# The first pair of weight steps of each feed-forward layer computed without the seven-product scheme

## The reference, cut to what matters

```python
def swiglu(u, wg, wu, wd):
    return (jax.nn.silu(u @ wg) * (u @ wu)) @ wd

for l in range(DEPTH):                       # DEPTH = 2
    hp = hp + 0.5 * swiglu(rms_norm(hp, norm_ffn1[l]), ffn1_wg[l], ffn1_wu[l], ffn1_wd[l])
    ...
    hp = hp + mp                             # mixer A and B in layer 0, a pooling mixer in layer 1
    hp = hp + 0.5 * swiglu(rms_norm(hp, norm_ffn2[l]), ffn2_wg[l], ffn2_wu[l], ffn2_wd[l])
```

## Time and profile before

| | before |
|---|---|
| median of 3 runs | 1993.95 us (1992.81 to 1995.24) |
| span of the profiled execution | 1990.5 us |
| PE busy | 1886.5 us, 95% |
| DVE / ACT / POOL busy | 69% / 61% / 41% |
| matmuls | 14529 |

### The profile page before, as it was taken

How to read it: one execution, slowest core, us unless ns; L and a number is a source line. 1 busy time by engine, 2 the same in 40 slices (tenths; PEclk the granted TensorE clock), 3 DMA queues, 4 the chain that set the end, 5 groups by cost and what they waited for, 6 DMA issues and landing times. The chain is left out here.

```text
span 1990.5 us, 37093 instructions
## 1 busy us (share of the span) xinstructions
PE 1886.5 (95%) x14529; PEld 1431.9 (72%) x14531; DVE 1377.3 (69%) x2159; ACT 1220.6 (61%) x1509; POOL 813.3 (41%) x520
## 2 busy tenths in 40 slices
PE   5999999999999889899999998999999989999999
PEld 2677777776668747677777775777777667777777
DVE  8767863467998866777876367768753787788532
ACT  5677787744933375577785346777743347778631
POOL 5666521112545132566640046666300457675000
PEclk8999999999999999999999999999999999999999
DMA  3222337612110021122222221223322012232330
GB/s 146 85 106 85 106 141 266 255 47 75 59 43 26 35 85 43 43 97 93 106 101 92 87 82 64 87 103 106 123 97 79 22 46 106 106 107 93 117 115 22
DMA packets 29170, 183.96 MB, mean 92 GB/s; under 512 B 3600, under 2 KB 4080, under 8 KB 13440
## 3 DMA queue, kind: packets, MB, share of 16 engines
q1 hardware_dynamic: 22896, 161.08, 22.6%
q0 software_dynamic: 6160, 21.34, 2.9%
HBM read 178.58 MB, written 3.83 MB: 92 GB/s over the span
## 5 line engine op out<-in xcount | busy, mean ns | idle before, releaser
L2404 PE MATMUL ps<-big 128*128 128x296 f16 (+1 forms) x2464 | 717.2, 291 | 31.3 <-DVE big L1535 12.0
L2410 PE MATMUL ps<-big 128*128 128x296 f16 (+1 forms) x2464 | 716.8, 291 | 15.8 <-DVE big L1412 14.3
L2405 PE MATMUL ps<-big 128*128 128x296 f16 (+1 forms) x2464 | 716.8, 291 | 0.0
L2386 PE MATMUL ps<-big 128*128 128x296 f16 (+1 forms) x4296 | 549.1, 290 | 7.6 <-POOL big L551 3.3
L2386 PEld LDWEIGHTS ps<-big 128*128 128x128 f16 x4296 | 415.4, 98 | 132.7 <-DVE big L1543 4.4
L467 POOL TENSOR_TENSOR big<-big 128x512 f32<-128x512 f32 x88 | 122.0, 1386 | 500.4 <-ACT big L734 245.8
L2404 PEld LDWEIGHTS ps<-big 128*128 128x128 f16 x2464 | 242.1, 98 | 111.1 <-DVE big L1535 15.0
L2410 PEld LDWEIGHTS ps<-big 128*128 128x128 f16 x2464 | 242.0, 98 | 92.5 <-DVE big L1412 21.2
L2405 PEld LDWEIGHTS ps<-big 128*128 128x128 f16 x2464 | 242.3, 98 | 66.2 <-issue 0.3
L1535 DVE SCALAR_TENSOR_TENSOR big<-big,scales 128x2048 f16<-128x2048 f32 x88 | 246.3, 2799 | 9.8 <-ACT big L753 9.4
L745 ACT ACTIVATE big<-big,scales 128x1536 f16<-128x1536 f32 x88 | 138.6, 1575 | 181.1 <-PE ps L2410 132.2
(11 more groups left out here) (354 smaller groups left out, 2636.9 us busy)
## 6 DMA issues: line engine op xcount, KB each, us to landing
big<-in_w_up SPq DMA_DIRECT2D x88, 1024.0 KB, 4.7
big<-in_w_dn SPq DMA_DIRECT2D x32, 1408.0 KB, 5.9
big<-in_w_in POOLq DMA_DIRECT2D x20, 512.0 KB, 6.0
big<-in_w_in SPq DMA_DIRECT2D x20, 512.0 KB, 3.3
big<-in_w_out POOLq DMA_DIRECT2D x8, 512.0 KB, 6.3
big<-in_w_out SPq DMA_DIRECT2D x1, 4096.0 KB, 12.1
resid<-in_x SPq DMA_DIRECT2D x4, 592.0 KB, 6.1
out_y<-resid SPq DMA_DIRECT2D x8, 296.0 KB, 4.7
```

The source lines that it names most:

```text
L2386: last = mm(ps[:, bank + hf, 0:n], w, x[:, hf * HALF:hf * HALF + n], start=start, stop=stop)
L2404: mm(out, w[:, 0, c], xop[:, 0, x, c, 0:FFN_COLS[f]], start=start, stop=False, skip_group_check=True)
L2405: mm(out, w[:, 1, c], xop[:, 0, x, c, 0:FFN_COLS[f]], start=False, stop=False, skip_group_check=True)
L2410: last = mm(out, w[:, 0, c], xop[:, 1, x, c, 0:FFN_COLS[f]], start=False, stop=(c == DC // 2 - 1), skip_group_check=True)
```

## The change

`FAST` stays for pairs 1 to 10. The first pair (steps u=0 and u=1) no longer uses the seven products. Each step is now 4 quarters x 2 token halves = 8 half-size products of 12 matmuls, 96 per step and 192 per pair instead of 168. PE's new function `plain` runs them:

```diff
+                def plain(h, b, groups, signal=None, n=0):
+
+                    w = w16[:, b, :, 0:4 * QW].rearrange("p a (q c n) -> p a q c n", q=4, c=DC // 2)
+                    out = [ps[:, bank, 0:FFN_COLS[f]] for bank in ((0, 2), (3, 4), (5, 6), (3, 4))[2 * h + b]]
+                    for g in groups:
+                        side, k = g // 2, g % 2
+                        x = (7, 3)[side] if h else side
...
+                        if h and b and g == 0:
+                            pe.wait_ge(hid1_done, PAIRS * f + 1)
+                            pe.wait_ge(hid2_done, PAIRS * f + 1)
+                        pe.wait_ge(x_high, 16 * f + X_AT[x] + k + 1)
+                        for c in (2 * k, 2 * k + 1):
...
+                            for m in range(2):
+                                for part in range(2):
+                                    mm(out[m], w[:, part, PLAIN[m, side], c], high, start=(g == 0 and c == 0 and part == 0),
+                                       stop=False)
+                        low_wait(f, x, k)
+                        for c in (2 * k, 2 * k + 1):
...
-                halves = stage != 0
-                order = [(0, "P1"), (0, "P2"), (1, "P1"), (1, "P2")] if stage in (3, 5) else \
-                    [(0, "P1"), (1, "P1"), (0, "P2"), (1, "P2")]
...
-                    first_step(b, name)
-                unit_total(stage, 3, 1)
-                with pe.Fori(1, HEAD_PAIRS) as i:
+                plain(0, 0, (0, 1))
+                if stage:
+                    sums(stage, 1)
+                plain(0, 1, (0, 1))
+                if stage:
+                    spread_half(stage, 1)
+                plain(0, 0, (2, 3), prod_done[0], 3)
+                plain(0, 1, (2, 3), prod_done[1], 3)
+                plain(1, 0, (0, 1))
+                plain(1, 1, (0, 1))
+                plain(1, 0, (2, 3), prod_done[0], 4)
+                unit_total(stage, 2, 0)
+                plain(1, 1, (2, 3), prod_done[1], 4)
+                pe.wait_ge(silu_done, PAIRS * f + 1)
+                unit_total(stage, 3, 1)
+                pair(1)
+                with pe.Fori(2, HEAD_PAIRS) as i:
                     pair(i)
```

The first argument of `plain` is the token half, the second the step (0 gate, 1 up); groups 0 and 1 are feature chunks 0 to 3, groups 2 and 3 chunks 4 to 7. The second token half of the up step shares banks 3 and 4 with the first half, so it waits until DVE has multiplied them out. The 24 `idle_products` are gone. Around this, on the other engines:

```diff
 # POOL
             def ffn(stage, next_stage=None):
 
-                if stage:
-                    first_lows(FFN_OF_STAGE[stage])
+                first_lows(FFN_OF_STAGE[stage])
                 mix_weights(stage, 2, 0)
                 mix_x(FFN_OF_STAGE[stage])
-                for u in range(3, FC):
+                mix_weights(stage, 3, 1)
+                mixed_low(FFN_OF_STAGE[stage])
+                for u in range(4, FC):
                     mix_weights(stage, u, u % 2)
...
-                if next_stage:
-                    first_two(next_stage)
 # ACT, first_turn
-                for b in range(2):
-                    if b or stage == 0:
-                        seed_p1(f, 0, b, FIRST)
-                x_highs(f, 2)
+                x_highs(f, 7)
                 x_highs(f, 3)
...
-                silu_first(f, 0, FIRST)
-                for b in range(2):
-                    keep_p5(f, 0, b, FIRST)
+                x_highs(f, 2)
+                plain_silu(f, 0)
                 x_highs(f, 4)
                 x_highs(f, 5)
-                keep_u2(f, 0, 0, FIRST)
+                bound(stage, 3, 1)
+                plain_silu(f, 1)
+                step_high1(stage, 2, 0)
+                step_high2(stage, 2, 0)
                 x_highs(f, 6)
...
 # DVE, x_rest
-                for k in range(2):
-                    scale_x(stage, 2 * k, 1)
-                    scale_x(stage, 2 * k + 1, 1)
-                    mix(0, k)
...
+                for c in range(DC):
+                    scale_x(stage, c, 1)
...
+                for k in range(2):
+                    x_low_of(stage, 3, k)
+                for t in range(2):
+                    for k in range(2):
+                        mix(t, k)
+                for k in range(2):
+                    x_low_of(stage, 2, k)
+                plain_hidden(f, 0)
+                for k in range(2):
+                    mix(2, k)
+                for k in range(2):
+                    x_low_of(stage, 4, k)
+                weight_scale(stage, 2, 0)
+                step_low1(stage, 2, 0)
+                step_low2(stage, 2, 0)
+                for k in range(2):
+                    x_low_of(stage, 5, k)
```

More of the change, by code:

```diff
@@ L744, in step_high1 @@
                     act.wait_ge(part_mm, DC * f - 1 + u)
-                a.activation(w16[:, b, 0, 0:3 * QW], wslot[:, b, QW:STEP_W], ACT.Copy, scale=wscale[:, b:b + 1]) \
+                first = 0 if isinstance(u, int) and u < 2 else QW
+                a.activation(w16[:, b, 0, 0:3 * QW], wslot[:, b, first:first + 3 * QW], ACT.Copy, scale=wscale[:, b:b + 1]) \
                     .then_inc(whigh1_done, 1)
@@ L2306, in _ @@
             step_low1(5, 0, 0)
+            step_low2(5, 0, 0)
             def next_updates():
```

226 lines of the change are left out of this document (120 added, 106 removed).

## The result

The changed kernel takes **2021.9 us** (median of 4 runs, 2021.0 to 2023.1) where the kernel before takes 1993.7 in the same comparison: a ratio of **1.0142 (95% interval 1.0127 to 1.0156)**, slower by 28 us. I had forecast 1982.7. The profiled execution has a span of 2019.8 us against 1990.5, 29.3 us more, and it is this difference that is taken apart here.

The account below looks back on a forecast made before the run. PE was taken to bound the kernel, 95% busy, with gains in the FFN heads, ended by ACT/DVE weight preparation. Heads: 11.1 - 1.6 + 3.5 + 3.4 = 16.4, less 5.1 for clock: 1993.95 - 11.3 = 1982.7 us, range 1973 to 1993.

Parts of the forecast that it names:

- waits for banks 3 and 4: PE's new wait before the up step's second token half, until DVE's plain_hidden: 3.4 us in FFN 1 to 3, 0.4 in FFN 0.
- low clock, behind the waits and behind E: Three more low-clock stretches of 3.4 us over the heads, half lost each: 5.1 us. E is P6's first matmul, pair 1.
- the four tails: From step 0's last product to E (P6's first matmul, pair 1): 12.3 us per head, 11.8 in FFN 3.
- T0 of FFN 0: First product of FFN 0's head: at 22.0 us, 2.5 earlier than before.
- Eight operations on x: 7.8 us: DVE's work ahead of freeing the banks: four low parts at 1.10 us and four sums at 0.85, the earlier group means.
- POOL has only four sums and two low parts there: Argument against DVE and POOL taking turns at the eight operations ahead of the banks.
- the slower rival: DVE and POOL take turns at the eight operations, 1.97 us each; wait 7.9 us longer per head, 2014 us; chance 0.10.
- Two low parts of operand 5: 2.0 us: DVE's low parts, new in the tail between step_low2 of step 2 and the scale of step 3: 2.0 us.
- from E on nothing differs: Sign for the new profile: no change after E, the first matmul of P6 in pair 1, step 0.
- a low stretch lasts 3.4 us: Expected length of PE's low-clock stretches, half of it lost each time; bounds none and 3.4 us per head.
- The head of FFN 1: From first product T0 to E: 25.6 + 12.3 = 37.9 us against 36.3 before, 1.6 lost.
- the twelve us of products: 24 added matmuls in each of four first pairs, 0.126 us each: 12.1 us more PE work, against the waits.

Follow-up runs that it names:

- e11: Changed kernel with one line moved: POOL forms step 2's sums ahead of operand 7's low parts, with no new wait; 2010.5 us.
- e2: Changed kernel with one wait more: POOL starts step 2's sums only after the first pair's SiLU products (hid2_done); 1993.6 us.
- e3: Changed kernel with weight_back of step 2 and the scale of step 3 on DVE ahead of operand 5's low parts and the memset; 2009.3 us.
- e6: Changed kernel with the edits of e2 and e3 together; 1984.7 us.
- e10: e6 with POOL's step 2 sums ahead of operand 7's low parts, step 3's ahead of mix_x, and SiLU products ahead of operand 2's low parts; 1981.2 us.
- e7: e6 with POOL's sums of step 3 also delayed, until behind step_low2 of step 2; 1990.0 us.
- e8: e7 with SiLU products right behind DVE's first two low parts, and POOL waiting for x's fourth low part instead of the products; 1997.7 us.

## Why the prediction was wrong

The forecast's span was 1990.5 - 11.3 = 1979.2 us, the measured one 2019.8: 40.6 us apart. In the forecast's own terms:

| term | forecast | measured | difference |
|---|---|---|---|
| waits for banks 3 and 4 (0.4 + 3 x 3.4) | 10.6 | 32.3 | +21.7 |
| low clock, behind the waits and behind E | 5.1 | 16.2 | +11.1 |
| the four tails | 48.7 | 53.6 | +4.9 |
| T0 of FFN 0, and the way to the banks | | | +0.9 |
| stretches that the change does not touch | 0 | 1.8 | +1.8 |

The lines add up to 40.4; the rest is rounding.

- **"Eight operations on x: 7.8 us" is the term that failed.** It measured 13.0 (1.62 us each, above the 1.33 from which the change was said to lose). The means of the earlier trace rows came from heads in which POOL stood idle, or was itself held, beside most of these operations. They are means over operations at full pace (0.72 to 0.78 us, as 814.98 above) and operations that took turns with POOL (up to 1.97), and I used them without asking which of the two the new place would be. The wait of PE followed one for one: 8.5 instead of 3.4 us, and 6.8 instead of 0.4 in FFN 0.
- **"POOL has only four sums and two low parts there" was the reason given against the slower rival, and it did not count against it.** Four sums of step 2, two sums of x and the end of a low part, with turns on each, cover all eight operations. I had not followed POOL's queue past the new `first_lows`, although the row of its idle time and the line of the diff were both at hand. e11 puts the sums back and regains 4.3 us in the eight; e2 takes all of POOL but operand 7's low parts away and regains 6.8.
- **The slower rival had the mechanism right and the size nearly.** It said turns at 1.97 us, a wait 7.9 us longer, and 2014 us. It was 5.1 us longer in three heads and 6.4 in FFN 0. The time went above 2014 through what the rival left out: operand 5's low parts and the clock. A chance of 0.10 was too low for it. The rule of the Trainium skill (SBUF — State Buffer, Who interferes with whom) would have made this rival the forecast. The trace agrees with the rule in direction, with 13.0 us beside POOL against 6.2 in e2, where only operand 7's low parts stand beside the first of the eight. It does not show a complete exclusion, and it shows DVE at full pace beside POOL as well (814.98 in the kernel before): from 820.22 to 825.53 us POOL did three sums (3.8 us at 1.26) and DVE about three and a half operations (2.6 us at 0.73), together 6.4 us of work in 5.3, an estimate from the rows above. The scalings, with one input in PSUM, kept to 3.56 us for eight beside POOL's 2.58 us of low parts, as it also says.
- **"Two low parts of operand 5: 2.0 us"** measured 3.67, by the same error. With the rest of the tail near its forecast (step_low1 1.82 for 2.1, step_low2 2.35 for 2.7), the tail of FFN 1 was 853.20 - 839.62 = 13.6 us for 12.3.
- **The clock** was forecast at 5.1 us and cost 16.2. In FFN 1 the first twelve matmuls behind the wait ran at the 1.2 GHz level (0.246 us apart) and cost 1.9 us with what followed; behind the four waits it was 7.5 us together, behind the four E 8.7. The second place was the wrong one: I expected "from E on nothing differs". PE had idled 5.09 us in front of E, and in e3, where it idles 0.94, the clock behind E stays high. That a low stretch lasts 3.4 us was a size without a row: the earlier trace rows show one low stretch, of 6.80 us. What it was meant to price, 1.7 us per place, measured 1.3 to 2.7.
- The head of FFN 1 in these terms: 37.9 forecast + 5.1 (wait) + 1.9 (clock behind it) + 1.3 (tail) = 46.2; measured 46.28. The rest stood: T0 of FFN 0 at 22.75 (forecast 22.0), PE at the banks 16.3 us behind T0 (16.2), the scalings' start, and the twelve us of products that were to be paid for out of the old waits: e2, with every product of the change, is level with the kernel before, and e6 and e10 are below it.
- The wait alone does not mend the forecast. In e2 PE waits 5.4 us for the banks, less than the 10.6 forecast, and its time of 1993.6 is still 11 us above 1982.7. The tail had to be shortened too: e6 comes to 1984.7.

What stays open: 1.8 us of the difference lie in stretches with the same code. Why DVE and POOL take turns in one place and one of them is held in another isn't shown. A kernel in which POOL's sums of steps 2 and 3 both stand in its idle time wasn't tried; in FFN 0 and 2 the load of step 2 has only just landed there.

## What to carry to other kernels

A mean duration from a profile belongs to its neighbours. Before an operation of DVE with both inputs in SBUF is priced in a new place, lay POOL's timeline beside that place. In this kernel such an operation of 592 columns was worth 0.75 us where POOL was idle; where POOL worked it was anything from 0.72 us, with POOL held, to 1.97, and the forecast has to carry both ends as its range. When a helper at the front of an in-order queue gets an operand that comes later, everything behind it moves too; look for what had used the idle time. And give each experiment that delays one engine the question of when its own results are due: e7 and e8 lost to that.

## What the runs showed that I had not expected

One sum of POOL took 5.16 us while DVE ran six operations at full pace, and in the changed kernel both engines were slowed (POOL 1.6 to 1.8 us for 1.26, DVE 1.6 for 0.75). The runs do not show what decides between the two. In e10 POOL's sum began 0.15 us behind an operation of DVE both times: in FFN 1 it was held over six operations, in FFN 0 the engines took turns from the second operation on. In e2 POOL began 0.16 us behind DVE (818.88 and 818.72 us) and they took turns as well; in e8 (820.65 and 820.50) POOL was held, for 3.79 us.

The low clock behind E came after an idle time of PE of 4.5 to 5.1 us in the changed kernel and cost 1.3 to 2.7 us of the 48 matmuls there. In e3, after 0.94 us, it did not come. The idle time just before is not the whole of it: in FFN 2 of e6 the clock fell within the twelve matmuls behind an idle time of 2.22 us, and was still low behind the next one, of 1.35 us. The profile shows the low clock only as longer matmuls (0.45 us for 0.29), never as a wait, so it has to be added to a forecast wait by hand.
